# Norms over two ranges of tokens, squares added in pairs on GpSimd, modulation sums taken two at a time

## The reference

```python
for i in range(2):                       # first block, two layers
    y = mla_mixer(...) if i == 0 else dsa_mixer(...)
    x = layer_norm(ALPHA * x + y, ln_g[i, 0], ln_b[i, 0])            # ln0, ln3
    y = memory_cross_attention(x, mem, ...)
    x = layer_norm(ALPHA * x + y, ln_g[i, 1], ln_b[i, 1])            # ln1, ln4
    y = swiglu_ffn(x, ffn_w_in[i], ffn_w_down[i])
    x = layer_norm(ALPHA * x + y, ln_g[i, 2], ln_b[i, 2])            # ln2, ln5
mod = c_act @ mod_w + mod_b              # second block, one layer: six vectors
h = rmsnorm(x, norm1_g) * (1 + sc1) + sh1                            # rms1
x = x + g1 * (concat(fox_attention(h), pool(h)) @ w_out)
h = rmsnorm(x, norm2_g) * (1 + sc2) + sh2                            # rms2
x = x + g2 * conv_ffn(h, ffn_up, ffn_conv_w, ffn_conv_b, ffn_down)
return rmsnorm(x, final_g)                                           # rms3
```

## Time and profile before

| what | value |
|---|---|
| median of 3 runs | 2419.61 us (2419.35 to 2431.77) |
| the profiled execution | 2422.34 us, span 2420.5 us |
| PE busy | 2317.2 us (96%), mean granted clock 0.981 |
| DVE busy | 1246.4 us (51%) |
| ACT busy | 1010.3 us (42%) |
| POOL busy | 160.8 us (7%) |
| HBM | 87 GB/s over the span |

### The profile page before, as it was taken

How to read it: one execution, slowest core, us unless ns; L and a number is a source line. 1 busy time by engine, 2 the same in 40 slices (tenths; PEclk the granted TensorE clock), 3 DMA queues, 4 the chain that set the end, 5 groups by cost and what they waited for, 6 DMA issues and landing times.

```text
span 2420.5 us, 47668 instructions
## 1 busy us (share of the span) xinstructions
PE 2317.2 (96%) x18858; PEld 2134.7 (88%) x18862; DVE 1246.4 (51%) x2504; ACT 1010.3 (42%) x1555; POOL 160.8 (7%) x186
## 2 busy tenths in 40 slices
PE   7999999999999989889999999999989998999998
PEld 7966899899999978756899989999969787999997
DVE  5467344455553146999453455553154644656412
ACT  4556254243332143756353343332153535555413
POOL 1000100100000040135100100000030000000000
PEclk9999999999999999899999999999999999999999
DMA  6333242344552222100242235543212202333220
GB/s 161 82 74 83 83 146 69 87 112 132 137 149 99 102 63 70 37 19 1 70 157 70 71 105 136 150 130 122 87 44 87 76 18 70 89 103 96 95 104 35
DMA packets 307592, 219.02 MB, mean 90 GB/s; under 512 B 42698, under 2 KB 294544, under 8 KB 307472
## 3 DMA queue, kind: packets, MB, share of 16 engines
q1 hardware_dynamic: 255792, 189.30, 26.2%
q10 hardware_dynamic: 49920, 25.17, 4.0%
q0 software_dynamic: 1760, 2.88, 0.4%
HBM read 207.56 MB, written 2.10 MB: 87 GB/s over the span
## 4 chain that ended last, share of the span: by engine, by line
PE 90%; ACT 5%; DVE 3%; issue 1%; DMA 0%; POOL 0%; SPq 0%; DVEq 0%; ACTq 0%; POOLq 0%
PE bank L637 72%; PE bank L779 5%; PE bank L749 3%; PE bank L713 3%; PE bank L879 1%; PE bank L1094 1%; PE bank L937 1%; PE bank L929 1%; ACT ST L1510 1%; PE bank L1143 1%; ACT XH L1180 1%; ACT XT L1354 1%; ACT BI L1180 1%; DVE SC L1963 1%; ACT WH L600 0%
## 5 line engine op out<-in xcount | busy, mean ns | idle before, releaser
L637 PE MATMUL bank<-XH,WH 128*128 128x256 f32 x3568 | 1003.3, 281 | 33.0 <-DVE XL L1828 24.4
L637 PE MATMUL bank<-XL,WH 128*128 128x256 f32 x3568 | 996.7, 279 | 0.0
L637 PE MATMUL bank<-XH,WL 128*128 128x256 f32 x3568 | 996.5, 279 | 0.0
L637 PEld LDWEIGHTS bank<-XH,WH 128*128 128x128 f32 x3568 | 678.7, 190 | 41.9 <-issue 32.1
L637 PEld LDWEIGHTS bank<-XH,WL 128*128 128x128 f32 x3568 | 676.1, 189 | 0.0
L637 PEld LDWEIGHTS bank<-XL,WH 128*128 128x128 f32 x3568 | 675.1, 189 | 0.2 <-issue 0.2
L604 DVE TENSOR_TENSOR WL<-RAW,WH 128x2048 fp32r<-128x2048 f32 x172 | 394.2, 2292 | 525.8 <-ACT WH L600 525.8
L600 ACT ACTIVATE WH<-RAW 128x2048 fp32r<-128x2048 f32 x172 | 328.6, 1911 | 445.7 <-PE bank L637 445.5
L637 PE MATMUL bank<-HH,WH 128*128 (+1 forms) x1056 | 295.2, 280 | 0.9 <-DVE HF L1908 0.9
L637 PE MATMUL bank<-HH,WL 128*128 (+1 forms) x1056 | 294.9, 279 | 0.0
L637 PE MATMUL bank<-HL,WH 128*128 (+1 forms) x1056 | 294.9, 279 | 0.0
(11 more groups left out here) (304 smaller groups left out, 3168.3 us busy)
## 6 DMA issues: line engine op xcount, KB each, us to landing
RAW<-in_ffn_w_in SPq DMA_DIRECT2D x88, 512.0 KB, 5.0
MB<-in_mod_w ACTq DMA_DIRECT2D x48, 512.0 KB, 5.2
RAW<-in_ffn_w_down SPq DMA_DIRECT2D x44, 512.0 KB, 3.9
RAW<-in_ffn_up SPq DMA_DIRECT2D x44, 512.0 KB, 4.5
RAW<-in_xa_w_kv SPq DMA_DIRECT2D x32, 512.0 KB, 4.4
RAW<-in_ffn_down SPq DMA_DIRECT2D x22, 512.0 KB, 4.0
RAW<-in_xa_w_q SPq DMA_DIRECT2D x16, 512.0 KB, 4.0
RAW<-in_xa_w_o SPq DMA_DIRECT2D x16, 512.0 KB, 4.4
```

The costliest lines, as they stand in the source:

```text
L637: mm = nc.tensor.matmul(out_ap[:, cols], l, moving, start=(start and n == 0 and k == 0), stop=(stop and n == len(parts) - 1 and k == len(o ...
```

## The change

1. Tokens are divided into two ranges of 256 (`HALF`). Every step of the nine norms is done for one range at a time, by instructions of 256 columns where there was one of 512. `SQ` has room for eight squares per range.
2. The last two units of a projection (`skewed`) are computed first for range 0 of both, then for range 1; sums for the norm of range 0 (`inserts`) stand between the matmuls of range 1.
3. The first two units of the stage that follows (`halves_in`) are computed for range 0, then for range 1; sums for the norm of range 1 stand between the matmuls of range 0. After `ln0` and `ln3` they stand between the products of the memory.
4. In `ffn_down` each bank holds two channel tiles of one range. The last two units, 9 and 10, are computed together for range 0, then unit 9 and unit 10 for range 1. Unit 0 starts with four tiles of range 1.
5. POOL adds the squares in pairs (`pairs`), and PE sums four tiles per range. POOL adds the first six tiles of each range for the mean, and PE the last two.
6. `mod_sum` is called for two columns after every second unit. The last two columns are summed inside unit 0 of `ffn_down`, where they stood behind the norm.
7. After `rms3`, the transposes of range 0 stand ahead of the sum of range 1's squares.

The core of the diff:

```diff
+            def halves_in(name, xs, fill, between, behind=None):
+                t = TILE0[name]
+                slots = [(UNIT0[name] + u) % 2 for u in range(2)]
+                for h in range(2):
+                    for u in range(2):
...
+                        for n in range(DC):
+                            c = n
+                            if u == 0:
+                                pe.wait_ge(x_split, FILL0[fill] + 8 * h + n + 1)
...
+                            if h == 0 and (u, n) in between:
+                                between[u, n]()
...
+            def first_sums(stage, name):
+                if name[:2] == "ln":
+                    return {(2, 0): {8: lambda: proj_mean(stage, name, 0)}, (3, 0): {12: lambda: square_sum(name, 0)}}
+                return {(3, 0): {0: lambda: square_sum(name, 0)}}
+
+            def second_sums(name, mean):
+                if name[:2] == "ln":
+                    return {(0, 5): mean, (1, 7): lambda: square_sum(name, 1)}
+                return {(1, 3): lambda: square_sum(name, 1)}
...
-                    for n in (6, 7, 0, 1, 2, 3, 4, 5) if first else range(DC):
-                        if first and n == 0:
-                            pe.wait_ge(tile_free, TILE0[f"ffn_in{f}"] + 2 * FC)
-                        if first and n == 4 and f < DEPTH:
-                            pe.wait_ge(mod_out, MOD_N * f + MOD_N - 2)
...
+                    if first:
+                        pe.wait_ge(tile_free, TILE0[f"ffn_in{f}"] + 2 * FC)
+                    for c, h in [(c, 1) for c in (4, 5, 6, 7, 0, 1, 2, 3)] + [(c, 0) for c in range(DC)]:
+                        if first and (c, h) == (0, 1):
+                            last_sums()
+                        mm = products(i, j, c, h, first)
+                    mm.then_inc(unit_used, 1)
...
-                unit(9, 9, False, False)
-                unit(10, 10, False, True)
+                for i in (9, 10):
+                    wait_unit(name, i)
+                pe.wait_ge(hid_split, FC * f + FC)
+                for c in range(DC):
+                    products(9, 9, c, 0)
+                    mm = products(10, 10, c, 0, last=True)
...
+                def last_sums():
+                    if f < DEPTH:
+                        m = MOD_N * f + MOD_N - 2
+                        pe.wait_ge(mod_out, m)
+                        for par in range(2):
+                            mod_sum(m + par, par)
+                        pe.wait_ge(mod_out, m + 2)
...
+            def proj_norm(stage, name, gain=None, memory=None):
+                for u in range(2):
+                    for k in range(2):
+                        residual(stage, 2 * u + k, 0, gain)
+                    next_lo(dve, stage, u, u)
...
+                if name[:2] == "ln":
+                    centre(name, 0)
+                for c in (4, 5):
+                    residual(stage, c, 1, gain)
+                next_lo(dve, stage, 2, 2)
+                scale_and_low(name, 0, between={1: [lambda: residual(stage, 6, 1, gain)],
+                                                4: [lambda: residual(stage, 7, 1, gain)],
+                                                7: [lambda: next_lo(dve, stage, 3, 3)]})
...
+            def pairs(name, h):
+                i = PASS[name, h]
+                for m in range(4):
+                    pool.wait_ge(squared, 8 * i + 2 * m + 2)
+                    a = SQ[h][:, 2 * m, :]
+                    nc.gpsimd.tensor_tensor(a, a, SQ[h][:, 2 * m + 1, :], ALU.add).then_inc(sq_paired, 1)
```

More of the change, by code:

```diff
@@ L63, with proj_event, down_event, sum_banks @@
 FILLS = ["x0", "mla_o", "ln0", "xa0_o", "ln1", "ln2", "dsa_o", "ln3", "xa1_o", "ln4", "rms1", "fox_o", "rms2"]
-FILL0 = {n: 8 * i for i, n in enumerate(FILLS)}
-NORMS = ["ln0", "ln1", "ln2", "ln3", "ln4", "ln5", "rms1", "rms2", "rms3"]
-NORM_I = {n: i for i, n in enumerate(NORMS)}
-MEAN_TILES = [6 if n in ("ln2", "ln5") else 7 for n in NORMS[:6]]
-SUMMED = [sum(m - 1 for m in MEAN_TILES[:i + 1]) for i in range(6)]
+HALVED = ("ln0", "ln1", "ln2", "ln3", "ln4", "rms1", "rms2")
+FILL0, _f = {}, 0
+for _name in FILLS:
+    FILL0[_name] = _f
+    _f += 16 if _name in HALVED else 8
+NORMS = ["ln0", "ln1", "ln2", "ln3", "ln4", "ln5", "rms1", "rms2", "rms3"]
+LN_I = {n: i for i, n in enumerate(NORMS[:6])}
+HC = S // 2
+HALF = [slice(0, HC), slice(HC, S)]
+PASSES = [(n, h) for n in ("ln0", "ln1", "ln2", "ln3", "ln4") for h in range(2)]
+PASSES += [("ln5", 0), ("rms1", 0), ("ln5", 1), ("rms1", 1)] + [(n, h) for n in ("rms2", "rms3") for h in range(2)]
+PASS = {p: i for i, p in enumerate(PASSES)}
+def proj_event(c, h):
+    return c if c < 4 else 4 + 4 * h + (c - 4)
+def down_event(c, h):
+    return 4 * h + c // 2
+def sum_banks(name, h):
+    if name == "rms1":
+        return (None, 5 - h)
+    return (0, 1) if name in ("ln2", "ln5", "rms3") and h == 0 else (6, 7)
 COLS = {}
@@ L1003, in row_tiles @@
+                down_stage(f, sums, last_sums)
+            cross_attention(0, "mla_o")
+            feed_forward(0, "xa_o0", "ln1", "ln2")
             def row_tiles(tiles0, cols, n):
@@ L1366, in ln, with squares_of @@
-            def ln(idx, var_bank, hi=True, then=None, later=False):
-                def col(what):
-                    return lambda c: COL[:, bass.ds(c + (COLS[what] + 8 * idx), 1)]
-                return norm(f"ln{idx}", lambda c: (centred, 8 * idx + c + 1), var_bank, col("ln_g"), col("ln_b"), True, hi,
-                            ZB, then, later)
+            def squares_of(name, h, ready, src, which=range(DC)):
+                i = PASS[name, h]
+                if i >= 2:
+                    act.wait_ge(sq_summed, i - 1)
+                for n in which:
+                    act.wait_ge(*ready(n))
+                    nc.scalar.activation(SQ[h][:, n, :], src[:, n, HALF[h]], ACT.Square).then_inc(squared, 1)
@@ L2045, in _ @@
             hidden(1)
-            ln_down(5, 1, low=False)
+            down_norm("ln5", 1)
+            for n in range(DC):
+                scale("ln5", 0, n)
+            for m in range(4):
+                down_out(1, m, 1)
             dve.wait_ge(mod_out, 48)
@@ L2054, in _ @@
             dve.wait_ge(mod_out, 50)
-            norm("rms1", XT, None, None, ZB)
+            next_lo(dve, "ffn_down1", 10, 10)
+            centre("ln5", 1)
+            scale_and_low("rms1", 0)
+            for n in range(DC):
+                scale("ln5", 1, n)
+            scale_and_low("rms1", 1)
             for i in range(2):
@@ L2112, in _ @@
             attention("fox", 1, 8, 0.125, lambda g, i: cm(i % 4), o_lo("fox_o", x_hi0("fox_o") + 4))
-            proj_units("fox_o", gain=16)
-            norm("rms2", XT, None, None, ZB)
+            proj_norm("fox_o", "rms2", gain=16)
+            proj_norm_rest("rms2")
             hidden(2)
-            norm("rms3", XT, None, None)
+            for m in range(4):
+                down_out(2, m, 0)
+            for c in range(DC):
+                scale("rms3", 0, c)
+            for m in range(4):
+                down_out(2, m, 1)
+            for n in range(DC):
+                scale("rms3", 1, n)
         @block.gpsimd
@@ L2252, in _ @@
                     pool.dma_start(dst, F3[0:FOXH, sign, k, :]).then_inc(gates_in, 16)
+            for name in ("rms2", "rms3"):
+                for h in range(2):
+                    pairs(name, h)
 _INS = ["x", "mem", "positions", "rel_bias", "mla_w_in", "mla_q_norm", "mla_w_uq", "mla_kv_norm", "mla_w_ukv", "mla_w_o",
```

684 lines of the change are left out of this document (403 added, 281 removed).

## The result

| | kernel before | changed kernel |
|---|---|---|
| time, us (median) | 2425.1 (2419.4 to 2431.8) | 2463.5 (2458.5 to 2465.2) |
| ratio, 95% interval | 1 | 1.0166 (1.0130 to 1.0202) |
| profiled span, us | 2420.5 | 2456.7 |

The change makes the kernel 1.7% slower. The forecast, 2441.1 in a range of 2408 to 2457, had the direction and missed the size: measured 2463.5. Between the two spans lie +36.2 us, where the sum said +21.5. The other 7.7 of the 22.4 between 2441.1 and 2463.5 are the base: the forecast took off 2.7, by which the profiled execution before stood above its median, and the profiled execution of the changed kernel stands 5.0 under its own. The kernel before has a fourth time here, hence 2425.1 and not 2419.6.

The account below looks back on a forecast made before the run. PE bounds the kernel, holding 90% of what ended last, with 148 us of surplus around the norms to save. Terms -20.5 + 13.1 + 14.4 - 2 + 1 + 15.5 = +21.5, put on the median: 2441.1 us, range 2408 to 2457.

Parts of the forecast that it names:

- the sum: Whole kernel, all terms against the kernel before: -20.5 + 13.1 + 14.4 - 2 + 1 + 15.5 = +21.5 us.
- Ends: End of each of three ffn_down: PE waits 4.35 us for unit 10's weights ahead of unit 9; +13.1 us together.
- Starts: Start of ffn_down: PE waits 0.85 and 4.95 us in the first two, 2.8 in the third; +14.4 us together.
- ffn_in2's third unit: ffn_in2, behind rms2: PE waits 5.5 us more for the third unit's weights, split behind the convolution.
- The third unit of ffn_in0 and 1: Behind ln1 and ln4: range 1's first hidden tile is delayed by the second column's products, 1.5 us.
- The clock: Behind new long waits and hand-overs of PE the granted clock falls to the lower level: +15.5 us, bounds 0 and 28.
- seven stops: New long waits, three at ffn_down's ends, three at its starts, one in ffn_in2: 1.7 us of clock loss each, 11.9.
- Rival 1: At the new waits within dense work the clock holds: then +6, 2426 us; chance 0.27.
- The sums in twos: Modulation sums in ffn_in0 and 1: twos spare half of 44 changes of kind, about 0.1 us each: -2.
- rival 3: Dense matmuls of ffn_in2 and three ffn_down change pace: all slow +13, 2454 us; all fast 9 less; chance 0.13.
- The norms: All nine norms: PE's surplus time around them falls from 148 us to 127.7, 20.5 less.
- Rival 2: Norms vanish beneath dense work: 53 us less than forecast, 2388 us; half of it, 2414; chance 0.15.

Follow-up runs that it names:

- e11_before_twos: The kernel before with only the modulation sums of ffn_in0 and 1 two at a time behind every even unit: 2434.2 us, ratio 1.0059.
- e10_no_pairs: e5_four with modulation sums one behind each unit again and no pair adds on GpSimd, PE summing eight squares per range: 2420.6 us, ratio 0.9987.
- e5_four: Changed kernel with ffn_down's end and start reordered, unit 2's weights split earlier in ffn_in, rms3's output copies behind range 1's squares: 2403.3 us, ratio 0.9911.

## Why the prediction missed, step by step

**The new waits: right in place, nearly right in size.** Ends: 4.35 forecast, 4.37 measured, three times. Starts: 0.85 + 4.95 forecast, 0.93 + 4.00 and 0.93 + 3.91 measured in two; 2.8 forecast, 3.7 measured in the third. ffn_in2's third unit: 5.5 forecast, 5.68 measured.

**The third unit of ffn_in0 and 1: mis-sized.** Forecast 1.5, measured 3.90 and 3.98. The step "range 1's first hidden tile is delayed by the products" left out that ACT's load of modulation weights waits for those products, that a table load of 1.28 stands behind it, and that the split comes only behind the gate's whole chain. 4.9 us in two layers. The clock behind these two waits had no term at all, since seven stops were counted and these weren't among them: the units take 13.99 and 13.32 where 11.3 and 10.9 are due by their pace, another 5.1.

**The clock: right in kind, a stop's price too low.** I took 1.7 per long wait. Behind the waits at ffn_down's end 108 matmuls take 15.11 and 15.06 where 12.24 is due (108 x 0.1133). Behind the waits at its start 840 take 98.11 and 98.06 where 95.2 is due, and 864 take 100.92 where 97.9 is. That is 2.8 to 3.0 for each; the third ffn_down's end and the third units give 1.6 to 2.6. The seven stops of the forecast average some 2.6: 18, not 11.9, so the term was 6 low. The halving "I take half as spent on dense work" failed: behind these waits dense work follows at once, and of a low stretch of 6.8 us some 5.5 lie on it (849.2 to 856.0, PE back at 850.5). Rival 1, the clock holds, is refuted.

**The sums in twos: wrong in sign.** Forecast -2; ffn_in0 and 1 lost 0.41 in each of ten pairs of units, +8.3. This is rival 3's mechanism, but in the stages and by the cause that I didn't see, though the earlier trace rows had it: 11.42 and 11.01 alternate with each sum. I wrote "I can't derive which comes", where the timeline of the kernel before would have shown a turn at each of the 44 single sums. In total the pace was neutral in this pair of traces: ffn_down1 and 2 were slow before (124.50 for 1056, 121.83 for 1032) and fast after, -9.7. For ffn_down1 the rows under e11_before_twos say why it was slow before, and the change's wait at its start is what let it be fast after; why ffn_down2 was slow before no run shows. The forecast had none of this, and that it came out even was luck. e11_before_twos shows the part's own price: 12 us by the medians, 14 by the ratio.

**The norms: right where nothing is behind them, less elsewhere.** ln0 -1.7 (forecast -1.6). ln1 to the end of its second unit is 13.3 over dense time, where 14.6 was forecast. The stages with ln2 and with ln5 and rms1 come out 1 to 3 us short of their -4.2 and -4.0, with small stretches of lower clock in the hand-overs. In ln2 some of it is GpSimd's adds beside DVE's low parts, shown under e10_no_pairs; the forecast looked only at pair adds and low parts of one range, which indeed don't meet. In all its "+1, from 0 to 3" for GpSimd stands, as far as the rows tell. A sum of 256 columns, taken as 0.45, is 0.43 (1.73 for four at ffn_down2's end). GpSimd's pair add, taken as 0.74, is 0.84. The terms written out for ln1 add up to 16.5, not 16.1, and 148.0 less 127.7 is 20.3, not 20.5; with both put right the sum would have been +22.5. Rival 2, norms that vanish, is refuted: 13 waits for XL, 19.7 us, stand in the changed kernel and 19.8 still in e5_four.

Together: clock at the seven stops +6, third units +5 for the waits and +5 for the clock behind them, sums in twos +10, ffn_down's luck -10: about 17, where 14.7 us are missing. The rest, about -2, is a balance that is not taken apart further: ln2, ln5 with rms1, and rms2 come out 1 to 2 each above their forecasts, and ln1 with ln4, rms3 and the stretch to xa_o0 some 2 each below.

So the steps of the prediction that failed are three: the sums in twos, forecast at -2 and worth +8.3 in ffn_in0 and 1; the third units of ffn_in0 and 1, at 1.5 a layer and worth 3.9 and another 2.5 through the clock; and the price of a stop, at 1.7 and worth 2.6.

## What to carry to other kernels

A wait put ahead of work that used to cover it costs its own length and, with dense work on either side, more through the clock: here 1.6 to 3.0 us behind waits of 3.7 to 5.7. Four edits that moved only where waits and steps stand brought this kernel from 2463.5 to 2403.3. When one kernel change contains several parts, price each alone; here the pairs on GpSimd won 25 us, the two ranges, once their new waits were mended, neither won nor lost anything that can be told from nothing, and the sums in twos lost 8 or more. And look for two paces in equal groups of matmuls before calling the dense work fixed.
